# Turning the experts' hidden activations on VectorE instead of TensorE in an encoder layer's expert stage

## The chip, the cores and the metric

The kernel runs on one core of a Trainium2 chip. The metric is the device time of one launch in microseconds (us); lower is better. A core has TensorE (PE, matrix products; PEld is its weight load), VectorE (DVE), ScalarE (ACT), GpSimd (POOL) and SyncE (SP, which here only issues DMAs), each with a queue of its own that it works through in order; queues wait for each other by semaphores.

## The reference

One encoder layer for two groups of 1024 tokens of width 1024 (a mixer, then an expert-choice mixture of experts). The change touches the experts alone:

```python
def expert_choice_moe(h, w_router, w_gate, w_up, w_down):
    ...
    cap = EC_CAPACITY_FACTOR * n // N_EXPERTS          # 128 tokens per expert and group
    gate, idx = lax.top_k(aff.T, cap)
    xe = xf[idx]
    hid = jax.nn.silu(jnp.einsum('ecd,edf->ecf', xe, w_gate)) * jnp.einsum('ecd,edf->ecf', xe, w_up)
    ye = jnp.einsum('ecf,efd->ecd', hid, w_down) * gate[..., None].astype(h.dtype)
    y = jnp.zeros_like(xf).at[idx.reshape(-1)].add(ye.reshape(-1, D))
```

There are 16 experts with three 1024 x 1024 fp32 matrices each. The layer ends with x + gate2 * rmsnorm(y) per token.

## The kernel before

The function `experts` takes the second part of the run, from about 1240 us. Each product of fp32 matrices is made of three products of fp32r matrices: a value is split into a rounded high part and the rest, and hi*hi, hi*lo and lo*hi are added in PSUM. A weight matrix comes in four pieces (`NP`) of 256 rows, 1 MB each; there is one set of four piece buffers (`wf`, `w_hi`, `w_lo`) for all three matrices. SyncE loads a piece as soon as VectorE has split the piece before it in that buffer; ScalarE writes `w_hi` (L2397) as soon as TensorE is through with the piece before; VectorE writes `w_lo` (L2535). A piece is 24 matmuls of 128x128 by 512 columns (2 groups, 2 halves, 2 row blocks, 3 products), an expert 288.

TensorE's order for expert e (L2693 in `products`, body at the end of the file): UP of e, four pieces; the first two GATE pieces of e + 1; `turn_h` of e (L2713); the last two GATE pieces of e + 1; DOWN of e, four pieces. GATE and UP of an expert add into one half of `acc` (4 banks), and `j` switches halves from expert to expert.

The hidden activations `hid` are [token, feature] and must be [feature, token] for DOWN. ScalarE writes silu of GATE's sums into `hid` (L2420), VectorE multiplies UP's sums onto it (`multiply`, L2566). Then `turn_h` makes 16 transposes of 128x128 in four banks (1.75 us in all), ScalarE copies the banks as `h_hi` (L2404, `turned_out`), VectorE subtracts for `h_lo` (L2541). The gathered tokens `xe` take another way: VectorE's 32x32 block transpose (L2550, `turn_x`), with the rows gathered so that no block need change its partitions; it reads every eighth word. They are split at L2410 (ScalarE) and L2555 (VectorE).

VectorE's order in the body of expert e: `turn_x` of e + 1; splits of GATE pieces 1 and 2 of e + 1; `x_out`; GATE pieces 3 and 4; `multiply` of e; DOWN piece 1 of e; `mean` of two units; DOWN piece 2; `turned_out`; `result` of two units; DOWN pieces 3 and 4; UP pieces 1 and 2 of e + 1; `mean` and `result` of two more units; UP pieces 3 and 4. ScalarE's order: the same splits; `square` of two units behind DOWN piece 1; `silu` of e + 1 behind DOWN piece 4; `square` of two more behind UP piece 2; then UP pieces 3 and 4 and `weigh` (L2431, the gated output `ye`). GpSimd then adds `ye` to `y` in memory by a scatter (L2318).

A unit is 128 finished tokens to be normalised and stored: 26 in all. Experts 9 to 14 have four each (`window`), expert 15 two; all others have none. Units use two buffers, `fy` and `fx`, in turn: GpSimd loads two units (L2330, L2331; by indices from unit 16 on, in expert 13 and later, L2334, L2335), ScalarE squares them (L2443), VectorE makes the mean (L2570), GpSimd the root (L2345), VectorE the result (`result`, two instructions, L2578 and L2584), GpSimd stores it (L2352, L2358) and loads the next two only when that store has landed.

Experts 0 to 7 run in a hardware loop, two a pass; the last expert has an order of its own.

Of the kernel before, what the change touches and what calls it, by code (L numbers as in the profile page):

```python
# [5 lines left out]
F32 = mybir.dt.float32  # L6
F32R = mybir.dt.float32r
U32 = mybir.dt.uint32
ALU = mybir.AluOpType
# [2079 lines left out]
def experts(nc, io):  # L2089
# [13 lines left out]
    FIRST, UNITS = 8, 4  # L2103
    units = [(t // TT, t, None) for t in range(GROUPS * TT)]
# [14 lines left out]
    with ExitStack() as ctx:  # L2119
# [35 lines left out]
        h_hi = s.sb("h_hi", [P, GROUPS, KC, P], F32R)  # L2155
        h_lo = s.sb("h_lo", [P, GROUPS, KC, P], F32R)
# [24 lines left out]
        hid_ready = s.sem("hid_ready")  # L2181
        h_turned = s.sem("h_turned")
# [43 lines left out]
        def quarter_rows(g):  # L2226
            return xe[:, g, :].rearrange("p (t n) -> p t n", t=4)

# [161 lines left out]
        def _(act):  # L2390
# [20 lines left out]

            def silu(e, j, bs=range(BK)):
                if bs[-1] < BK - 1:
                    act.wait_ge(half_done, 1)
                else:
                    act.wait_ge(piece_done, ONE + piece(e, GATE, NP))
                if len(bs) == BK:
                    act.wait_ge(h_turned, ONE + e * BK)
                for b in bs:
                    nc.scalar.activation(hid[:, b // 2, b % 2 * HALF:(b % 2 + 1) * HALF], acc[:, j, b, :], ACT.Silu).then_inc(silu_ready, 1)  # L2420
# [36 lines left out]
            def body(e, j):  # L2457

                ns = window(e)
                if is_last(e):  # L2460
                    split(e, DOWN, range(0, 2))
                    turned_out(e, (h_hi, j), h_turned, h_hi_ready, range(0, 2))
                    split(e, DOWN, range(2, NP))
                    for n in ns:
                        square(n)
                    turned_out(e, (h_hi, j), h_turned, h_hi_ready, range(2, BK))
                else:
                    split(e + 1, GATE, range(0, 2))
                    x_out(e + 1, 1 - j)
                    split(e + 1, GATE, range(2, NP))  # L2470

                    split(e, DOWN, range(0, 1))
                    for n in ns[0:2]:
                        square(n)
                    split(e, DOWN, range(1, 2))
                    turned_out(e, (h_hi, j), h_turned, h_hi_ready)
                    split(e, DOWN, range(2, NP))

# [16 lines left out]
        def _(dve):  # L2495
# [61 lines left out]

            def multiply(e, j, bs=range(BK)):
# [42 lines left out]
            def body(e, j):  # L2601
                ns = window(e)
                if is_last(e):
                    multiply(e, j, range(0, 2))
                    split(e, DOWN, range(0, 2))
                    turned_out(e, h_hi, h_lo, j, h_hi_ready, h_ready, range(0, 2))
# [4 lines left out]
                    turned_out(e, h_hi, h_lo, j, h_hi_ready, h_ready, range(2, BK))  # L2611
                    for n in ns:
                        result(n)
                else:
# [50 lines left out]
        def _(pe):  # L2665
# [42 lines left out]
            def turn_h(e, j, bs=range(BK)):  # L2708
                pe.wait_ge(hid_ready, ONE + e * BK + bs[-1] + 1)
                for b in bs:  # L2710
# [3 lines left out]
                    mm.then_inc(h_turned, 1)  # L2714
# [12 lines left out]
            def body(e, j):  # L2727
                first, second = range(0, 2), range(2, NP)
                pe.wait_ge(silu_ready, ONE + e * BK + 2)
                if is_last(e):  # L2730
# [7 lines left out]
                    pe.wait_ge(h_ready, ONE + e * BK + 2)  # L2738
# [3 lines left out]
                    pe.wait_ge(h_ready, ONE + e * BK + BK)  # L2742
                    for b in bs[1]:
                        products(e, DOWN, j, h_hi, h_lo, bs=range(b, b + 1))
                else:
# [7 lines left out]
                    turn_h(e, j)  # L2753
                    products(e + 1, GATE, 1 - j, x_hi[:, 1 - j], x_lo[:, 1 - j], second)
                    pe.wait_ge(h_ready, ONE + e * BK + BK)
                    products(e, DOWN, j, h_hi, h_lo)
# [82 lines left out]
```

## Time and profile before

| | us |
|---|---|
| median of 3 runs | 2374.05 |
| lowest and highest | 2373.64, 2375.26 |
| the profiled execution's own time | 2373.01 |
| its span | 2371.2 |
| TensorE busy | 2267.5 (96%) |
| VectorE busy | 1265.4 (53%) |
| ScalarE busy | 1102.7 (47%) |
| GpSimd busy | 743.5 (31%) |

The span is that of the one profiled execution; its own time holds 1.8 us more around the span. Matmuls are pipelined: a row shows one as busy for 0.39 us while the next starts 0.23 us later, so busy shares of TensorE say little, and the steps between starts are what to read. Idle time of an engine that is not the bottleneck costs nothing by itself.

### The profile page before, as it was taken

The page shows a single profiled execution, that of the slowest core. Times are in us where ns is not written, and L with a number is a line of the kernel's source. Part 1 is how long each engine was busy: PE and PEld are TensorE (multiplying, and loading weights), DVE is VectorE, ACT ScalarE, POOL GpSimd, SP SyncE. Part 2 cuts the span into 40 slices and gives each one's busy share as a digit, 9 for nine tenths or more (in the row PEclk, how much of TensorE's full clock was granted, in tenths as well). Part 3 has the DMA queues.
Part 4 walks back from the last instruction along what each step waited for, and adds up shares of the span by engine and source line. Part 5 has one row for each costly group of instructions (what it writes and reads, how often), then busy time and mean ns, then how long its engine had stood idle before and what let it go on. Part 6 is the DMA issues. An engine that isn't in the chain of part 4 may idle for free. (4 is left out here: it accounts for less than half of the span.)

```text
span 2371.2 us, 34817 instructions
## 1 busy us (share of the span) xinstructions
PE 2267.5 (96%) x13347; PEld 1890.4 (80%) x13347; DVE 1265.4 (53%) x1883; ACT 1102.7 (47%) x1798; POOL 743.5 (31%) x770
## 2 busy tenths in 40 slices
PE   6999999999999999999975999999999999999997
PEld 4679989877899898667754888888888888888886
DVE  3212344555423445656557665555555566777665
ACT  4222444655434436665543444444444445555543
POOL 3004241444132415440013333221223323433634
PEclk9999999999999999999997999999999999999999
DMA  8835445657554459764537667666667679988785
GB/s 317 265 110 181 152 151 187 187 152 175 137 182 152 151 179 258 208 200 157 172 140 283 230 226 230 217 218 210 209 222 235 228 254 325 329 303 302 292 322 177
DMA packets 224095, 511.49 MB, mean 216 GB/s; under 512 B 38420, under 2 KB 129444, under 8 KB 204496
## 3 DMA queue, kind: packets, MB, share of 16 engines
q1 hardware_dynamic: 174576, 394.78, 49.4%
q0 software_dynamic: 49376, 114.78, 16.4%
q8 instruction: 92, 1.51, 0.3%
q14 instruction: 51, 0.42, 0.1%
HBM read 415.32 MB, written 93.69 MB: 215 GB/s over the span
## 5 line engine op out<-in xcount | busy, mean ns | idle before, releaser
L2535 DVE TENSOR_TENSOR moe_w_lo<-moe_wf,moe_w_hi 128x2048 fp32r<-128x2048 f32 x192 | 438.8, 2289 | 369.7 <-ACT moe_w_hi L2397 369.1
L2397 ACT ACTIVATE moe_w_hi<-moe_wf 128x2048 fp32r<-128x2048 f32 x192 | 368.0, 1917 | 524.3 <-PE moe_acc L2693 524.1
L2693 PE MATMUL moe_acc<-moe_w_hi,moe_x_hi 128*128 128x512 f32 x1024 | 400.7, 391 | 0.9 <-DVE moe_x_lo L2541 0.6
L2693 PE MATMUL moe_acc<-moe_w_hi,moe_x_lo 128*128 128x512 f32 x1024 | 399.1, 390 | 0.0
L2693 PE MATMUL moe_acc<-moe_w_lo,moe_x_hi 128*128 128x512 f32 x1024 | 398.9, 390 | 0.0
L2693 PEld LDWEIGHTS moe_acc<-moe_w_hi,moe_x_hi 128*128 128x128 f32 x1024 | 192.3, 188 | 40.8 <-DVE moe_x_lo L2541 0.8
L2693 PEld LDWEIGHTS moe_acc<-moe_w_hi,moe_x_lo 128*128 128x128 f32 x1024 | 192.3, 188 | 40.0
L2693 PEld LDWEIGHTS moe_acc<-moe_w_lo,moe_x_hi 128*128 128x128 f32 x1024 | 192.4, 188 | 39.3
L1793 PE MATMUL banks<-fr_w_hi,fr_h_hi 128*128 128x256 f32 x768 | 223.5, 291 | 0.0
L1793 PE MATMUL banks<-fr_w_lo,fr_h_hi 128*128 128x256 f32 x768 | 217.3, 283 | 0.0
L1793 PE MATMUL banks<-fr_w_hi,fr_h_lo 128*128 128x256 f32 x768 | 217.3, 283 | 0.0
L2301 POOL DMA_INDIRECT moe_xe<-scratch_h,moe_parts x120 | 187.5, 1562 | 85.9 <-issue 76.3
L1784 PE MATMUL banks<-fr_h_hi,fr_w_hi 128*128 128x512 f32 x496 | 204.5, 412 | 1.9 <-DVE fr_h_lo L1381 1.1
L2693 PE MATMUL moe_acc<-moe_w_hi,moe_h_hi 128*128 128x512 f32 x512 | 199.5, 390 | 0.0
L2693 PE MATMUL moe_acc<-moe_w_hi,moe_h_lo 128*128 128x512 f32 x512 | 199.4, 389 | 0.0
L2693 PE MATMUL moe_acc<-moe_w_lo,moe_h_hi 128*128 128x512 f32 x512 | 199.4, 389 | 0.0
L1784 PE MATMUL banks<-fr_h_hi,fr_w_lo 128*128 128x512 f32 x496 | 194.4, 392 | 0.0
L1784 PE MATMUL banks<-fr_h_lo,fr_w_hi 128*128 128x512 f32 x496 | 193.9, 391 | 0.0
L1030 ACT ACTIVATE fr_stage<-banks 128x512 f32<-128x512 f32 (+1 forms) x114 | 67.3, 590 | 272.0 <-PE banks L1784 146.9
L906 POOL DMA_DIRECT2D fr_v<-scratch_vov x224 | 156.5, 743 | 81.6 <-PE banks L1963 80.2
L1362 DVE TENSOR_TENSOR fr_w_lo<-fr_w_raw,fr_w_hi 128x1024 fp32r<-128x1024 f32 x56 | 71.7, 1282 | 206.0 <-ACT fr_w_hi L1018 206.0
L1793 PEld LDWEIGHTS banks<-fr_w_hi,fr_h_hi 128*128 128x128 f32 x768 | 147.0, 191 | 4.9 <-issue 4.8
(303 smaller groups left out, 4191.9 us busy)
## 6 DMA issues: line engine op xcount, KB each, us to landing
moe_wf<-in_w_expert_gate SPq DMA_DIRECT2D x64, 1024.0 KB, 5.0
moe_wf<-in_w_expert_up SPq DMA_DIRECT2D x64, 1024.0 KB, 4.9
moe_wf<-in_w_expert_down SPq DMA_DIRECT2D x64, 1024.0 KB, 6.9
fr_w_raw<-in_w_units SPq DMA_DIRECT2D x28, 1024.0 KB, 6.7
fr_bias<-in_na_bias SPq DMA_DIRECT2D x16, 1520.0 KB, 11.0
fr_a_w<-in_w_ada POOLq DMA_DIRECT2D x16, 1024.0 KB, 8.3
scratch_qk_t<-fr_stage SPq DMA_DIRECT2D x64, 256.0 KB, 2.5
scratch_vov<-fr_stage SPq DMA_DIRECT2D x96, 128.0 KB, 2.4
```

What stands on the lines that cost most here:

```text
L906: pool.dma_start(v[j][p0:CHUNK, CH_AT[rb] + n, :], v_view[2, m, r0:r0 + k, cols_, :]).then_inc(nv_loaded[j], 16)
L1030: nc.scalar.activation(out, product, ACT.Copy).then_inc(evac_done, 1)
L1362: nc.vector.tensor_tensor(w_lo[:, h % 2, k, :], w_raw[:, h % 2, k, :], w_hi[:, h % 2, k, :].bitcast(F32), ALU.subtract).then_inc(w_lo_read ...
L1784: mm = nc.tensor.matmul(ps[:, b % 2, :], w[x1][:, slot, k, a * P:(a + 1) * P], h[x2][:, k, t * HALF:(t + 1) * HALF], start=start, stop=stop)
L1793: mm = nc.tensor.matmul(ps[:, b % 2, part * QW:(part + 1) * QW], h[x1][:, k, tile:tile + P], w[x2][:, slot, k, :], start=(k == 0 and i == ...
L2301: pool.indirect_dma_start(quarter_rows(g)[:, t, :], None, h2_quarters, bass.IndirectOffsetOnAxis(ap=at, axis=0)).then_inc(gathered[g], 16)
L2397: nc.scalar.activation(w_hi[:, q, :, :], wf[:, q, :, :], ACT.Copy).then_inc(w_hi_ready, 1)
L2535: nc.vector.tensor_tensor(w_lo[:, q, :, :], wf[:, q, :, :], w_hi[:, q, :, :].bitcast(F32), ALU.subtract).then_inc(w_lo_ready, 1)
L2693: mm = nc.tensor.matmul(acc[:, j, b, :], x[:, g, k, :], w[:, q, a, h * HALF:(h + 1) * HALF], start=(k == 0 and i == 0), stop=(k == KC - 1 ...
```

## The change

For all experts but the last (`LATE` = 15), `hid` is turned by VectorE with its 32x32 block transpose. Each instruction turns 16 blocks: it reads one quarter of the partitions (32 tokens) and, of each 128 features, one group of 32, and writes them to another quarter of the partitions (the 32 features) of `h_raw`. Sixteen instructions (4 quarters by 4 groups) make the whole, with a drain ahead. `h_raw` lies at the same address as `h_lo`. ScalarE copies it to `h_hi` from SBUF in two instructions of 1024 columns (`h_out`), and VectorE subtracts for `h_lo` in two. `turn_h` of TensorE is gone for these experts. VectorE's order changes: `multiply` moves ahead of the split of GATE's fourth piece, and the turns stand behind that split and ahead of DOWN's first. DOWN's first piece on TensorE is reordered: all its products with `h_hi` first, under a wait for `h_hi` alone, then those with `h_lo`. The last expert keeps the old way under semaphores of its own.

```diff
+    LATE = 15
...
+        with nc.sbuf_tensor("moe_h_raw", [P, GROUPS, KC, P], F32) as h_raw:
+            pass
         h_lo = s.sb("h_lo", [P, GROUPS, KC, P], F32R)
...
             (ScalarE)
+            def h_out(e):
+
+                act.wait_ge(h_turned, ONE + e + 1)
+                for g in range(GROUPS):
+                    nc.scalar.activation(h_hi[:, g, :, :], h_raw[:, g, :, :], ACT.Copy).then_inc(h_hi_ready, 1)
...
                     split(e, DOWN, range(0, 1))
+                    if not is_late(e):
+                        h_out(e)
                     for n in ns[0:2]:
                         square(n)
                     split(e, DOWN, range(1, 2))
-                    turned_out(e, (h_hi, j), h_turned, h_hi_ready)
+                    if is_late(e):
+                        turned_out(e - LATE, (h_hi, j), late_h_turned, late_h_hi_ready)
                     split(e, DOWN, range(2, NP))
...
             (VectorE)
+            def turn_h(e):
+                dve.drain()
+                for t in range(4):
+                    for u in range(4):
+                        columns = hid[t * QT:(t + 1) * QT, :, :].rearrange("r g (m u c) -> r g m u c", m=KC, u=4)[:, :, :, u, :]
+                        a = nc.vector.transpose(h_raw[u * QT:(u + 1) * QT, :, :, t * QT:(t + 1) * QT], columns)
+                a.then_inc(h_turned, 1)
+
+            def h_out(e):
+                for g in range(GROUPS):
+                    dve.wait_ge(h_hi_ready, ONE + e * GROUPS + g + 1)
+                    nc.vector.tensor_tensor(h_lo[:, g, :, :], h_raw[:, g, :, :], h_hi[:, g, :, :].bitcast(F32),
+                                            ALU.subtract).then_inc(h_ready, 1)
...
-                    split(e + 1, GATE, range(2, NP))
-                    multiply(e, j)
+                    if is_late(e):
+                        split(e + 1, GATE, range(2, NP))
+                        multiply(e, j)
+                    else:
+                        split(e + 1, GATE, range(2, 3))
+                        multiply(e, j)
+                        split(e + 1, GATE, range(3, NP))
+                        turn_h(e)
                     split(e, DOWN, range(0, 1))
+                    if not is_late(e):
+                        h_out(e)
                     for n in ns[0:2]:
                         mean(n)
                     split(e, DOWN, range(1, 2))
-                    turned_out(e, h_hi, h_lo, j, h_hi_ready, h_ready)
+                    if is_late(e):
+                        turned_out(e - LATE, h_hi, h_lo, j, late_h_hi_ready, late_h_ready)
                     for n in ns[0:2]:
                         result(n)
...
             (TensorE)
+            def down_first(e, j):
+                pe.wait_ge(w_lo_ready, ONE + piece(e, DOWN, 0) + 1)
+                pe.wait_ge(h_hi_ready, ONE + (e + 1) * GROUPS)
+                for x, ws in ((h_hi, (w_hi, w_lo)), (h_lo, (w_hi,))):
+                    if x is h_lo:
+                        pe.wait_ge(h_ready, ONE + (e + 1) * GROUPS)
+                    for b in range(BK):
+                        for a in range(PIECE):
+                            for w in ws:
+                                mm = nc.tensor.matmul(acc[:, j, b, :], x[:, b // 2, a, :], w[:, 0, a, b % 2 * HALF:(b % 2 + 1) * HALF],
+                                                      start=(a == 0 and w is w_hi and x is h_hi), stop=False)
+                mm.then_inc(piece_done, 1)
...
-                    turn_h(e, j)
+                    if is_late(e):
+                        turn_h(e, j)
                     products(e + 1, GATE, 1 - j, x_hi[:, 1 - j], x_lo[:, 1 - j], second)
-                    pe.wait_ge(h_ready, ONE + e * BK + BK)
-                    products(e, DOWN, j, h_hi, h_lo)
+                    if is_late(e):
+                        pe.wait_ge(late_h_ready, ONE + (e - LATE) * BK + BK)
+                        products(e, DOWN, j, h_hi, h_lo)
+                    else:
+                        down_first(e, j)
+                        products(e, DOWN, j, h_hi, h_lo, range(1, NP))
```

## Rows read from the trace of the kernel before

**Rows 1.** Chain that ended last: start us, us, engine, tile and line.

```profile
1338.76 1.75 PE moe_acc L2713 x16
1340.51 65.33 PE moe_acc L2693 x288
...
2210.59 1.75 PE moe_acc L2713 x16
```

**Rows 2.** Busy time of each engine in two stretches of 67 us.

```profile
1546.00:1613.00 67.00, 67.00 (x306) 55.71 (x305) 38.52 (x26) 31.10 (x26) 17.82 (x13) 1.00 0.67 219
1948.00:2015.00 67.00, 67.00 (x305) 55.72 (x304) 48.54 (x37) 35.72 (x34) 25.50 (x26) 1.00 0.87 314
```

**Rows 3.** Groups by line and shape: count, busy us, mean ns, idle before.

```profile
L2550 DVE STREAM_TRANSPOSE moe_x_raw<-moe_xe 128x1024 f32<-128x1024 f32 x30 | 63.0, 2140 | 0.0
L2541 DVE TENSOR_TENSOR moe_h_lo<-moe_acc,moe_h_hi 128x512 fp32r<-128x512 f32 x64 | 39.7, 683 | 0.3 <-ACT moe_h_hi L2404 0.3
L2555 DVE TENSOR_TENSOR moe_x_lo<-moe_x_raw,moe_x_hi 128x1024 fp32r<-128x1024 f32 x30 | 35.4, 1222 | 0.0
...
L2404 ACT ACTIVATE moe_h_hi<-moe_acc 128x512 fp32r<-128x512 f32 x64 | 32.7, 594 | 0.0
L2410 ACT ACTIVATE moe_x_hi<-moe_x_raw 128x1024 fp32r<-128x1024 f32 x30 | 29.8, 1042 | 0.0
```

**Rows 4.** Timeline around the multiply of expert 3 (start us, us).

```profile
1533.27 2.47 DVE L2566 TENSOR_TENSOR moe_hid<-moe_hid,moe_acc 128x512 f32<-128x512 f32 x4
1536.51 2.29 DVE L2535 TENSOR_TENSOR moe_w_lo<-moe_wf,moe_w_hi 128x2048 fp32r<-128x2048 f32 x1 [0.76 <-ACT moe_w_hi L2397]
```

**Rows 5.** Timelines of ScalarE, VectorE and GpSimd in expert 9.

```profile
1931.56 1.92 ACT L2397 ACTIVATE moe_w_hi<-moe_wf 128x2048 fp32r<-128x2048 f32 x1 [3.52 <-PE moe_acc L2693]
...
1939.00 1.06 ACT L2443 ACTIVATE moe_zero<-moe_fy 128x1024 f32<-128x1024 f32 x1
...
1941.20 0.18 ACT L2443 ACTIVATION_READ_ACCUMULATOR moe_zero<-moe_fy 128x1 f32 x1
...
1948.98 1.28 DVE L2578 SCALAR_TENSOR_TENSOR moe_fy<-moe_fy,moe_parts,moe_rows 128x1024 f32<-128x1024 f32 x1
1950.34 1.23 DVE L2584 TENSOR_TENSOR moe_fx<-moe_fx,moe_fy 128x1024 f32<-128x1024 f32 x1
...
1957.62 0.53 POOL L2330 DMA_DIRECT2D moe_fy<-scratch_y  x1 [1.40 <-DMA out<-moe_fx]
...
1970.96 1.28 DVE L2578 SCALAR_TENSOR_TENSOR moe_fy<-moe_fy,moe_parts,moe_rows 128x1024 f32<-128x1024 f32 x1
```

**Rows 6.** Two lines' instructions: duration ns min/median/max.

```profile
L1661 DVE SCALAR_TENSOR_TENSOR fr_r<-fr_nd x8: 181/187/1301, 268.9 to 873.6; 128x16 f32<-128x16 f32 x8
...
L1575 DVE SCALAR_TENSOR_TENSOR fr_scale<-fr_mods,fr_g_pre x2: 158/163/168, 35.0 to 35.1; 128x8 f32<-128x8 f32 x2
```

**Rows 7.** VectorE's timeline in experts 13 and 14.

```profile
2217.24 1.28 DVE L2578 SCALAR_TENSOR_TENSOR moe_fy<-moe_fy,moe_parts,moe_rows 128x1024 f32<-128x1024 f32 x1
...
2242.43 1.28 DVE L2578 SCALAR_TENSOR_TENSOR moe_fy<-moe_fy,moe_parts,moe_rows 128x1024 f32<-128x1024 f32 x1 [0.91 <-POOL moe_parts L2345]
...
2247.43 4.49 DVE L2535 TENSOR_TENSOR moe_w_lo<-moe_wf,moe_w_hi 128x2048 fp32r<-128x2048 f32 x2
...
2255.92 4.48 DVE L2535 TENSOR_TENSOR moe_w_lo<-moe_wf,moe_w_hi 128x2048 fp32r<-128x2048 f32 x2
...
2284.29 1.28 DVE L2578 SCALAR_TENSOR_TENSOR moe_fy<-moe_fy,moe_parts,moe_rows 128x1024 f32<-128x1024 f32 x1
...
2309.13 1.28 DVE L2578 SCALAR_TENSOR_TENSOR moe_fy<-moe_fy,moe_parts,moe_rows 128x1024 f32<-128x1024 f32 x1
```

**Rows 8.** Transfers of tile `moe_fy`, loads of units.

```profile
DMA to landing us min/median/max: 4.8/8.4/11.1
```

**Rows 9.** Timeline of the end: the last matmul, VectorE behind it.

```profile
2357.03 0.39 PE L2693 MATMUL moe_acc<-moe_w_hi,moe_h_lo 128*128 128x512 f32 x1
...
2357.45 0.75 DVE L2647 SCALAR_TENSOR_TENSOR moe_xe<-moe_acc,moe_parts,moe_xe 128x512 f32<-128x512 f32 x1
```

More of the change, by code:

```diff
@@ L2181, in experts @@
         hid_ready = s.sem("hid_ready")
+        late_h_turned, late_h_hi_ready, late_h_ready = (s.sem(f"late_h_{n}") for n in ("turned", "hi_ready", "ready"))
         h_turned = s.sem("h_turned")
@@ L2227, in quarter_rows, with is_late @@
             return xe[:, g, :].rearrange("p (t n) -> p t n", t=4)
+        def is_late(e):
+            return isinstance(e, int) and e >= LATE
         def is_last(e, n=1):
@@ L2416, in silu @@
                     act.wait_ge(piece_done, ONE + piece(e, GATE, NP))
-                if len(bs) == BK:
-                    act.wait_ge(h_turned, ONE + e * BK)
+                if len(bs) == BK and is_late(e - 1):
+                    act.wait_ge(late_h_turned, ONE + (e - LATE) * BK)
+                elif len(bs) == BK:
+                    act.wait_ge(h_turned, ONE + e)
                 for b in bs:
@@ L2461, in body @@
                     split(e, DOWN, range(0, 2))
-                    turned_out(e, (h_hi, j), h_turned, h_hi_ready, range(0, 2))
+                    turned_out(e - LATE, (h_hi, j), late_h_turned, late_h_hi_ready, range(0, 2))
                     split(e, DOWN, range(2, NP))
@@ L2465, in body @@
                         square(n)
-                    turned_out(e, (h_hi, j), h_turned, h_hi_ready, range(2, BK))
+                    turned_out(e - LATE, (h_hi, j), late_h_turned, late_h_hi_ready, range(2, BK))
                 else:
@@ L2605, in body @@
                     split(e, DOWN, range(0, 2))
-                    turned_out(e, h_hi, h_lo, j, h_hi_ready, h_ready, range(0, 2))
+                    turned_out(e - LATE, h_hi, h_lo, j, late_h_hi_ready, late_h_ready, range(0, 2))
                     multiply(e, j, range(2, BK))
@@ L2610, in body @@
                         mean(n)
-                    turned_out(e, h_hi, h_lo, j, h_hi_ready, h_ready, range(2, BK))
+                    turned_out(e - LATE, h_hi, h_lo, j, late_h_hi_ready, late_h_ready, range(2, BK))
                     for n in ns:
@@ L2713, in turn_h @@
                         mm = nc.tensor.transpose(acc[:, j, b, k * P:(k + 1) * P], hid[:, b // 2, c * P:(c + 1) * P], ident[:, :])
-                    mm.then_inc(h_turned, 1)
+                    mm.then_inc(late_h_turned, 1)
+            def down_first(e, j):
[10 more added lines that the diff above has]
+                mm.then_inc(piece_done, 1)
             bs = [range(2 * g, 2 * g + 2) for g in range(GROUPS)]
@@ L2737, in body @@
                     products(e, UP, j, x_hi[:, j], x_lo[:, j], second, bs[1])
-                    pe.wait_ge(h_ready, ONE + e * BK + 2)
+                    pe.wait_ge(late_h_ready, ONE + (e - LATE) * BK + 2)
                     products(e, DOWN, j, h_hi, h_lo, first, bs[0])
@@ L2752, in body @@
                     products(e + 1, GATE, 1 - j, x_hi[:, 1 - j], x_lo[:, 1 - j], first)
-                    turn_h(e, j)
+                    if is_late(e):
+                        turn_h(e, j)
                     products(e + 1, GATE, 1 - j, x_hi[:, 1 - j], x_lo[:, 1 - j], second)
-                    pe.wait_ge(h_ready, ONE + e * BK + BK)
-                    products(e, DOWN, j, h_hi, h_lo)
+                    if is_late(e):
+                        pe.wait_ge(late_h_ready, ONE + (e - LATE) * BK + BK)
+                        products(e, DOWN, j, h_hi, h_lo)
+                    else:
+                        down_first(e, j)
+                        products(e, DOWN, j, h_hi, h_lo, range(1, NP))
             over_experts(pe, body)
```

## The prediction, made blind

> **What bounds the kernel now.** I read the chain that ended last, then the list of waits, then the timelines of the engines in the experts' stage. From 1339 us to the end TensorE has no wait worth naming: the chain shows 65.3 us of 288 matmuls per expert, 0.227 us each, then 1.75 us for the 16 transposes of `turn_h`, and again; the turns of experts 0 and 13 lie 871.83 us apart, so an expert takes 67.06 us [rows 1]. The stage is bound by how fast TensorE is fed instructions; all else is hidden, or late only from now on. VectorE is the next busiest: 38.5 of 67 us in a plain expert, 48.5 where finished tokens are also normalised (experts 9 to 14, "windows" below) [rows 2].
>
> **What the change removes.** The 16 turns leave TensorE for experts 0 to 14: 15 x 1.75 = 26.2 us, if nothing else becomes late. ScalarE trades four evictions for two copies of 1024 columns, VectorE four subtractions of 512 columns for two of 1024; in time that is even within 0.2 us [rows 3]. No DMA is added. The order of h_hi and h_lo products in the first DOWN piece changes no count of matmuls; it lets h_lo come 16 x 0.227 = 3.6 us later.
>
> **What it adds.** Sixteen VectorE transposes of 32 partitions x 512 columns per expert. Call the time from one start to the next t.
> - Columns set a VectorE duration: 512 take 683 ns, 1024 take 1222, 0.14 us plus 1.06 ns a column [rows 3]. In a run of four, starts lie about 0.60 us apart (2.47 us for four, the last 0.68 long) [rows 4]; where a drain stands between, a 1.28 us instruction is followed after 1.36 [rows 5], so 512 columns would take 0.77.
> - The one transpose row takes 2140 ns for 1024 columns [rows 3], 1.96 ns a column above the same 0.14: for 512, 1.14 us. But it reads every eighth word, where `turn_h` reads runs of 32 words. A read stride alone costs time here: 16 columns read 520 bytes apart take 187 ns, 8 in a dense form 163 [rows 6]; 16 dense ones would take 163 + 8 x 1.06 = 171, so the stride costs 1 ns a column. The transpose's excess over the dense rate is 0.90.
> So t lies between 0.60 and 0.77 at the dense rate, and at 1.14 at the row's own. I take 0.73, nearer the separated end: each transpose writes other partitions than the one before it, and no row shows such a pair overlapping.
>
> The Trainium skill ("VectorE: DVE Perf Modes", section "Two Vector instructions with no wait between them") says that an instruction whose output starts in another group of 32 partitions than the last output did is held until all earlier ones have finished. No run here shows it; by it the overlapped 0.60 is ruled out and t is 0.69 or more, while without it the sum below would be some 11 us lower. The same skill ("SBUF — State Buffer", the note on cachelines) says that reads which cross into a new 16-byte line each time pay a penalty; the transpose row agrees with its 2140 ns, and by it the dense rate holds.
>
> **A plain expert.** Let U be the end of its UP products; ScalarE's next split starts on it (for expert 9 at 1931.56 [rows 5]). VectorE now multiplies at once (2.4), splits the last GATE piece (2.2), drains (0.1), turns (16t), splits the first DOWN piece (2.2). That is U+7.0+16t. TensorE has four GATE pieces until U+21.8. No stall if t is under 0.92; at 0.73 the piece is there at U+18.7, 3 us early. ScalarE's h_hi, 2.0 us after the turns, is earlier still. All 1.75 us are kept: experts 0 to 8 give 9 x 1.75 = -15.7 us.
>
> **Windows.** Here the queue orders matter. Call R1 the start of the first pair of `result`, R2 of the second; between them lies a trip to memory (store the first pair, load into its buffers, square, mean, root). VectorE's order puts R1 behind the turns: multiply, split, turns, then on ScalarE h_hi 2.0, two squares 2.4 [rows 5] and the split of the second DOWN piece 1.9, with 0.1 at each handing over, then VectorE's 2.2. So R1 = U + 4.8 + 16t + 8.7 = U+25.2 at t = 0.73; before it is U+17.5 (1948.98 against 1931.5) [rows 5]. Everything behind R1 on VectorE moves with it, and GpSimd's stores wait for it.
> From R2 to the next R1, VectorE in program order: results 5.0, two splits 4.4, turn_x 4.1, two splits 4.4, x_lo 2.3, split 2.2, multiply 2.4, split 2.2, drain 0.1, turns 16t, then 8.7: 35.8 + 16t [rows 3, 4, 7] (the first step is 2247.43 - 2242.43, the next two 2255.92 - 2247.43 = 8.5 together).
> From R1 to R2, experts 9 to 12: the last load goes out 8.64 us after R1 [rows 5], lands 8.4 later (median) [rows 8], square 1.25, mean, root and their semaphores 1.0: 19.3. Before, VectorE's order hid it (22.0 us). In expert 13 the rows are scattered, and the trip is seen bare: 2242.43 - 2217.24 = 25.2 [rows 7].
> So R1 to R1 is 19.3 + 35.8 + 11.7 = 66.8 us in experts 9 to 12, where TensorE alone would need 65.3 and before took 67.06; and 25.2 + 35.8 + 11.7 = 72.7 from expert 13 to 14, where it took 67.05. TensorE follows, stalled at the third DOWN piece by 1 to 2 us an expert, and behind expert 13's R2 at the third UP piece and at x_lo.
> The end hangs on R1 of expert 14: its R2 comes some 25 us later, then the results' 5.0 and the split of expert 15's third UP piece, 2.2. Before, that piece was there at 2309.13 + 7.2 = 2316.3 [rows 7], and TensorE came to it at 2317.5 (turn of expert 14 at 2210.59 + 67.06, its 1.75, 168 matmuls); that 1 us is all there was to spare. After, R1 is 7.7 us and more later against U and TensorE's way is shorter by the turns: it waits 8 to 9 us. In the end VectorE's queue and the last matmul already meet within 0.2 us (2357.03 + 0.39 and 2357.45) [rows 9], so I let the end move by as much as R1 of expert 14.
>
> **The sum.** Experts 0 to 8 -15.7; R1 of expert 9 later against U by 25.2 - 17.5 = +7.7; four cycles of 66.8 for 67.06, -1.0; the cycle behind expert 13 +5.6. Total -3.4 us. Of 26.2 us won on TensorE the windows give back 23. Against the profiled execution: span 2371.2 - 3.4 = 2367.8, with 1.8 around it 2369.6; the median of the runs lies 1.04 above the profiled time: **2370.7 us**.
>
> **Rivals.**
> 1. *The transposes overlap* (t = 0.60): R1 is U+23.1, +5.6; the cycle would be 64.7, so TensorE's 65.3 rules and four experts give -7.0; expert 13's cycle is 70.6, less the 0.6 spare, +2.9. Sum -14.2: 2360. For it: neighbours on the same partitions overlap [rows 4]. Against: the changing partitions.
> 2. *The trip to memory gets longer*, and the kernel slower. The splits of third and fourth DOWN and first two UP pieces now run back to back, 2.2 us apart instead of 5.4, and each releases a 1 MB load just when the second pair's loads go out. Every us of landing adds 4: from 9.3 us nothing is won, from 10.5 the kernel is slower by 0.2%. At the slowest landing in the rows, 11.1 [rows 8], and t = 0.77: R1 to R1 70.1, four times +3.0; R1 of expert 9 +8.3; expert 13 +6.3; less 15.7: +11.1, 2385. Against: the queues already share the engines now with a median of 8.4.
> 3. *The turns run at the row's own rate*, t = 1.14. First DOWN piece at U+25.2, a stall of 3.4 in each plain expert, 9 x 1.7 = +15; R1 +14.3; four cycles of 73.3, +25; expert 13 +12.3: +67, 2441. For it: it is the only transpose row. Against: the strided rows account for it.
> 4. *The windows cost nothing* because the pair's results are reached in time by slack I don't see: -26.2, 2348. Against: program order on VectorE.
>
> **Chances.** Forecast (dense rate, held, trip as now, -9 to +5) 0.45; rival 1 0.22; rival 2 0.17; rival 3 0.13; rival 4 0.03. Outside 2359 to 2390 are rival 3 and rival 4, 0.16. The forecast's own range is 2365 to 2379. What this kernel's measurement can tell from no change is 0.2%, 4.7 us: faster takes rivals 1 and 4 and a quarter of the forecast, 0.36; same 0.30; slower 0.34.
>
> **What would show it.** The turned group on VectorE: 16 rows, each near 0.69 us, about 11.7 us together (9.6 or 18 for rivals 1 and 3). TensorE: in experts 0 to 8 no wait and starts 65.3 us apart; in windows waits for w_lo of 1 to 2 us; a wait of 8 to 9 us in expert 15's UP. R1 of expert 9 25 us behind U; R1 to R2 19 to 20 us. I am wrong if t is outside 0.69 to 0.77, if the loads' landing shifts by more than 1 us, or if the end follows something other than R1 of expert 14.

## The result and the profile after

The changed kernel takes 2380.87 us (median of 20 runs, 2377.24 to 2386.26); the kernel before took 2374.73 (median of 20, 2372.81 to 2383.17) on the same chips. The ratio is 1.0026 with a 95% interval of 1.002 to 1.0033: slower, just beyond the 0.2% that this measurement tells from no change. The forecast was 2370.7 us, a gain. The profiled execution has a span of 2377.3 us (own time 2379.06) against 2371.2 before, so the traces show 6.1 us to account for.

The chain that ended last, in the plain experts (start us, us, what; L2766 is `down_first`, L2734 all other products):

```profile
1350.73 5.44 PE moe_acc L2766 x24
1356.17 59.84 PE moe_acc L2734 x264
1416.01 5.44 PE moe_acc L2766 x24
...
1872.97 5.44 PE moe_acc L2766 x24
```

No transposes and no waits are left: (1872.97 - 1350.73) / 8 = 65.28 us an expert, where [rows 1] had 67.06. In the plain experts the change does all it promised.

One row of the groups by line, and VectorE's timeline in expert 3, which answer to [rows 3] and [rows 4]:

```profile
L2581 DVE STREAM_TRANSPOSE moe_h_raw<-moe_hid 32x512 f32<-32x512 f32 x240 | 168.7, 703 | 4.5
```

```profile
1524.85 2.48 DVE L2598 TENSOR_TENSOR moe_hid<-moe_hid,moe_acc 128x512 f32<-128x512 f32 x4 [1.14 <-PE moe_acc L2734]
1527.24 2.29 DVE L2553 TENSOR_TENSOR moe_w_lo<-moe_wf,moe_w_hi 128x2048 fp32r<-128x2048 f32 x1
1529.62 11.45 DVE L2581 STREAM_TRANSPOSE moe_h_raw<-moe_hid 32x512 f32<-32x512 f32 x16
1541.10 2.29 DVE L2553 TENSOR_TENSOR moe_w_lo<-moe_wf,moe_w_hi 128x2048 fp32r<-128x2048 f32 x1
1543.31 2.35 DVE L2587 TENSOR_TENSOR moe_h_lo<-moe_h_raw,moe_h_hi 128x1024 fp32r<-128x1024 f32 x2
```

A turn is 703 ns long and the sixteen take 11.45 us, 0.717 from start to start. `h_lo` is complete at 1545.66; TensorE comes to `down_first` at 1546.57, as the chain's steps of 65.28 from 1350.73 give. So even the products with h_lo would not have waited there.

Busy time of each engine in three stretches of 67 us, for [rows 2] (us, PE, PEld, DVE, ACT, POOL busy, granted clock, DMA share, GB/s). The first is plain, the second lies in expert 11's window, the third around expert 13's:

```profile
1545.00:1612.00 67.00, 67.00 (x297) 55.47 (x297) 51.14 (x40) 32.54 (x26) 16.14 (x13) 1.00 0.68 228
2082.00:2149.00 67.00, 63.98 (x280) 52.16 (x280) 56.75 (x49) 33.57 (x32) 26.10 (x26) 1.00 0.83 303
2216.00:2283.00 67.00, 60.84 (x257) 49.49 (x256) 53.58 (x45) 28.20 (x26) 29.76 (x20) 0.95 0.79 288
```

VectorE has 12.6 us more to do in the plain stretch (51.14 for 38.52 [rows 2]) and 8.2 more in the window (56.75 for 48.54), and TensorE now idles 3 to 6 us of 67. In the second row VectorE isn't full; it waits. The DMA engines are busy for 0.83 of it, but full engines alone don't stall TensorE: before, in a window, they were at 0.87 and 314 GB/s [rows 2] and TensorE had no idle time.

The list of waits for TensorE in this stage (engine, tile and line, waited for: us in total, times, longest us):

```profile
PE moe_acc L2734 <- DVE moe_w_lo L2553: 19.7, 7, 9.2
PE moe_acc L2734 <- DVE moe_x_lo L2573: 3.9, 4, 1.8
PE moe_acc L2734 <- ACT moe_hid L2435: 0.3, 1, 0.3
```

Now the trip from the first pair of results (R1) to the second (R2) in expert 11, on the timelines of VectorE, GpSimd and ScalarE:

```profile
2076.10 1.28 DVE L2610 SCALAR_TENSOR_TENSOR moe_fy<-moe_fy,moe_parts,moe_rows 128x1024 f32<-128x1024 f32 x1
...
2084.70 0.53 POOL L2337 DMA_DIRECT2D moe_fy<-scratch_y  x1 [1.03 <-DMA out<-moe_fx]
...
2088.58 1.06 ACT L2458 ACTIVATE moe_zero<-moe_fy 128x1024 f32<-128x1024 f32 x1 [4.36 <-DMA moe_fy<-scratch_y]
...
2096.93 1.06 ACT L2458 ACTIVATE moe_zero<-moe_fy 128x1024 f32<-128x1024 f32 x1 [7.20 <-DMA moe_fy<-scratch_y]
...
2098.12 0.15 DVE L2602 TENSOR_SCALAR moe_parts<-moe_parts 128x1 f32<-128x1 f32 x1 [8.07 <-ACT moe_zero L2458]
2098.19 1.27 DVE L2610 SCALAR_TENSOR_TENSOR moe_fy<-moe_fy,moe_parts,moe_rows 128x1024 f32<-128x1024 f32 x1
```

Read it as a sum: the second fy load goes out 8.60 us behind R1, its square starts 12.23 later (the landing), and R2 comes another 1.26 later: 22.09. ScalarE waits 4.4 and 7.2 us for these loads, VectorE 8.1 us for the square, with TensorE's splits queued behind both. In [rows 5] R2 came 22 us behind R1 too, but there nobody waited for it.

From the same timelines, in us (rows of before: [rows 5] and [rows 7]):

| | expert 9 | 10 | 11 | 12 | 13 | 14 |
|---|---|---|---|---|---|---|
| R1 before | 1948.98 | 2016.04 | 2083.11 | 2150.16 | 2217.24 | 2284.29 |
| R1 after | 1941.33 | 2008.81 | 2076.10 | 2145.30 | 2214.53 | 2288.49 |
| R1 to R2 after | 20.29 | 20.11 | 22.09 | 22.10 | 26.98 | 25.79 |
| R2 to next R1 after | 47.19 | 47.18 | 47.11 | 47.13 | 46.98 | |

The end: TensorE's long wait in expert 15's UP, and the granted clock behind it (timeline; stretches of 5 us as above):

```profile
2321.61 0.80 PE L2734 MATMUL moe_acc<-moe_w_hi,moe_x_hi 128*128 128x512 f32 x1 [9.17 <-DVE moe_w_lo L2553]
```

```profile
2316.00:2321.00 5.00, 0.00 (x0) 0.00 (x0) 4.92 (x4) 4.08 (x5) 1.82 (x1) 0.50 0.26 105
2321.00:2326.00 5.00, 4.39 (x11) 3.48 (x12) 2.76 (x2) 0.00 (x0) 3.56 (x2) 0.52 0.65 217
```

The granted clock is at its lower level, 1.2 GHz, in the last 5 us of the wait of 9.2 us and for about 4 us behind it: the first matmuls start 0.43 us apart where 0.227 is usual. From the matmul above to the transposes of expert 15 lie 48 matmuls; they take 12.98 us, and took 10.89 before.

### The profile page after: what moved, and what is told of

The parts are those of the page before. It is cut to its first block and busy times, and to the rows that moved or that the text cites. A ratio compares the mean times of both kernels' runs of the same rounds, so it can differ in the third digit from the quotient of the medians.

```text
span 2377.3 us, 34487 instructions
## 1 busy us (share of the span) xinstructions
PE 2249.0 (95%) x13107; PEld 1866.4 (79%) x13107; DVE 1424.3 (60%) x2093; ACT 1096.6 (46%) x1768; POOL 730.7 (31%) x770
## 5 line engine op out<-in xcount | busy, mean ns | idle before, releaser
L2734 PE MATMUL moe_acc<-moe_w_hi,moe_x_hi 128*128 128x512 f32 x1024 | 401.7, 392 | 19.0 <-DVE moe_w_lo L2553 14.1
L2734 PE MATMUL moe_acc<-moe_w_hi,moe_x_lo 128*128 128x512 f32 x1024 | 400.2, 391 | 0.0
L2734 PE MATMUL moe_acc<-moe_w_lo,moe_x_hi 128*128 128x512 f32 x1024 | 400.2, 391 | 0.0
L2734 PEld LDWEIGHTS moe_acc<-moe_w_hi,moe_x_hi 128*128 128x128 f32 x1024 | 193.4, 189 | 62.9 <-DVE moe_w_lo L2553 15.9
L2734 PEld LDWEIGHTS moe_acc<-moe_w_hi,moe_x_lo 128*128 128x128 f32 x1024 | 193.2, 189 | 40.5
L2734 PEld LDWEIGHTS moe_acc<-moe_w_lo,moe_x_hi 128*128 128x128 f32 x1024 | 193.4, 189 | 40.0
L2308 POOL DMA_INDIRECT moe_xe<-scratch_h,moe_parts x120 | 177.2, 1476 | 87.1 <-issue 77.5
L1030 ACT ACTIVATE fr_stage<-banks 128x512 f32<-128x512 f32 (+1 forms) x114 | 67.3, 590 | 270.3 <-PE banks L1784 145.4
L2581 DVE STREAM_TRANSPOSE moe_h_raw<-moe_hid 32x512 f32<-32x512 f32 x240 | 168.7, 703 | 4.5
L2734 PE MATMUL moe_acc<-moe_w_hi,moe_h_hi 128*128 128x512 f32 x392 | 153.2, 391 | 5.6 <-DVE moe_w_lo L2553 5.6
L2734 PE MATMUL moe_acc<-moe_w_lo,moe_h_hi 128*128 128x512 f32 x392 | 152.6, 389 | 0.0
L2734 PE MATMUL moe_acc<-moe_w_hi,moe_h_lo 128*128 128x512 f32 x392 | 152.6, 389 | 0.0
```

Of the source, the lines that this page charges most:

```text
L1030: nc.scalar.activation(out, product, ACT.Copy).then_inc(evac_done, 1)
L2308: pool.indirect_dma_start(quarter_rows(g)[:, t, :], None, h2_quarters, bass.IndirectOffsetOnAxis(ap=at, axis=0)).then_inc(gathered[g], 16)
L2581: a = nc.vector.transpose(h_raw[u * QT:(u + 1) * QT, :, :, t * QT:(t + 1) * QT], columns)
L2734: mm = nc.tensor.matmul(acc[:, j, b, :], x[:, g, k, :], w[:, q, a, h * HALF:(h + 1) * HALF], start=(k == 0 and i == 0), stop=(k == KC - 1 ...
```

## The experiments

Twelve kernels were run. Kernels of one group shared a chip and the runs of the kernel before (2374.08, 2374.42 and 2374.44 us in the three groups). Edits are against the changed kernel (2380.87) unless said. The first four ask: is it the windows, the last of them, the order, or the turn itself?

**late9: the turns on VectorE in plain experts alone.**

```diff
-    LATE = 15
+    LATE = 9
```

> The turns stay on VectorE in experts 0 to 8 alone; experts 9 to 14, whose windows normalise finished tokens, turn on TensorE as before. My theory (each plain expert keeps 1.75 us, all of the rest is lost in the windows): 9 x 1.75 = 15.7 us under the kernel before, 2359.0 us, and TensorE's cycle in the windows back at 67.05 us. Rival (the plain experts' gain is given back somewhere else, whatever the windows do, for instance by the loads that now come sooner): within 2 us of the kernel before, about 2375.

Measured: 2358.56 us, ratio to before 0.9934 (0.992 to 0.9948), 15.5 us under the kernel before. R1 of expert 10 and 11 are 2000.61 and 2067.66, 67.05 apart. The theory held: the plain experts' gain is whole, and the windows of the changed kernel lose all of it and 6 us more. One cycle is not back at 67.05: R1 of expert 13 to R1 of expert 14 takes 69.0, though nothing is turned on VectorE there. The next run shows why.

**late14: expert 14 turns on TensorE again** (`LATE = 14`).

> Expert 14 alone turns on TensorE again. Theory: the first pair of results of expert 14 comes some 7.7 us earlier against the end of its UP products, TensorE's 9.2 us wait in expert 15's UP shrinks by that, and TensorE gets 1.75 us of transposes more: 7.4 us under the changed kernel, 2373.5 us, equal to the kernel before. Rival (the end follows TensorE or the loads, not that pair): the turn's 1.75 us are added to the changed kernel, 2382.6.

Measured: 2379.11 us (1.002, 1.0011 to 1.0029). The theory missed by 5.6 us. R1 of expert 14 didn't come sooner: R2 of expert 13 to it takes 47.2 us with a queue that needs some 10 us less. The chain shows what takes that time:

```profile
2252.22 2.52 POOL scratch_y L2325
2255.05 11.63 DMA scratch_y<-moe_ye,moe_parts
2266.94 3.05 POOL moe_fy L2341
2270.29 0.97 POOL moe_fx L2342
2271.56 11.78 DMA moe_fy<-scratch_y,moe_parts
2284.57 1.81 ACT moe_w_hi L2404
2286.41 2.29 DVE moe_w_lo L2553
2289.30 1.79 DVE moe_h_lo L2559 x3
```

GpSimd stores expert 13's second pair, then adds an expert's rows to y (11.6 us), and only then may gather the next window's rows by index (11.8 us). Behind expert 13 a second chain, through GpSimd, is as long as VectorE's queue. My forecast had one chain there, though the chain of the kernel before already ran through the same two transfers:

```profile
2253.69 11.72 DMA scratch_y<-moe_ye,moe_parts
...
2268.24 8.19 DMA moe_fy<-scratch_y,moe_parts
```

**up_first: the second pair behind the last two UP splits**, on both engines; ScalarE's edit, VectorE's is alike:

```diff
-                    split(e + 1, UP, range(0, 2))
+                    split(e + 1, UP)
                     for n in ns[2:4]:
                         square(n)
-                    split(e + 1, UP, range(2, NP))
```

> Order alone is changed: on ScalarE and VectorE the second pair's square, mean and result come behind the splits of UP pieces 3 and 4 in place of ahead of them, so that these two splits (4.4 us on VectorE) fill the trip to memory between the first and the second pair. Theory (the windows lose because VectorE's queue has that trip in it with nothing to do, some 6 to 8 us of idle time each): the cycle falls from 67.3 to 69.2 us to about TensorE's own 65.3 in experts 9 to 12, five cycles give back 2 to 4 us each, and expert 15's third UP piece no longer waits for the results: between 2350 and 2362 us, first results still 25 us behind the end of UP. Rival A (the loads collide with weight loads, and the pair comes later still, whatever stands before it): 2375 to 2381. Rival B (VectorE is simply full with 58 of 65 us, order doesn't matter): 2380.

Measured: 2364.77 us (0.9957, 0.9943 to 0.997), 16 us under the changed kernel and 9 under before; that is 2.8 outside my span, on the theory's side of both rivals. R2 to next R1 is 42.8 in place of 47.2: exactly the two splits, 4.4 us. The trip grew to 23.6 to 24.2, since now the splits themselves wait (ScalarE in expert 11):

```profile
2090.47 1.92 ACT L2404 ACTIVATE moe_w_hi<-moe_wf 128x2048 fp32r<-128x2048 f32 x1 [6.93 <-DMA moe_wf<-in_w_expert_up]
2094.24 1.92 ACT L2404 ACTIVATE moe_w_hi<-moe_wf 128x2048 fp32r<-128x2048 f32 x1 [1.85 <-DMA moe_wf<-in_w_expert_up]
```

The cycles of experts 9 to 12 are 66.4 to 66.9 for 67.3 to 69.2. VectorE has 59 of 67 us of work here and that does no harm: rival B is out. Rival A named a true thing, late loads, and its number is wrong.

**u_outer: neighbouring turns write the same quarter.**

```diff
-                for t in range(4):
-                    for u in range(4):
+                for u in range(4):
+                    for t in range(4):
```

> The two loops of the 16 turns are exchanged: four turns in a row write the same quarter of the partitions, and only three of fifteen neighbours change it (before: all fifteen). The same work, the same result. Theory (a turn waits for the one before it because its output starts in other partitions): starts of neighbours in one quarter 0.60 us apart, the group 9.7 to 10 us instead of 11.45, the first pair of results 1.5 us earlier against U, the kernel 4 to 8 us faster than the changed one, about 2375. Rival (the 0.717 us are what 512 columns of a transpose cost, wherever they go): 11.4 us for the group, 2381.

```profile
1530.99 11.45 DVE L2581 STREAM_TRANSPOSE moe_h_raw<-moe_hid 32x512 f32<-32x512 f32 x16
```

Measured: 2381.71 us (1.0029, 1.0019 to 1.0039); the sixteen again take 11.45 us. Both numbers are the rival's, but the run doesn't decide for it. The exchange moves the change of partitions from one side to the other: in the changed kernel neighbours read the same quarter and write different ones; here they write the same quarter, and each reads another one than its neighbour (`t` is the inner loop). So all fifteen neighbours still differ in partitions on one side. What is shown is that equal output partitions alone bring nothing.

Whether the turns would overlap with equal partitions on both sides stays open, and other rows speak for it. The two transposes of the gathered tokens read and write all partitions, one behind the other (expert 9 of the changed kernel):

```profile
1971.01 2.23 DVE L2568 STREAM_TRANSPOSE moe_x_raw<-moe_xe 128x1024 f32<-128x1024 f32 x1
1973.15 2.13 DVE L2568 STREAM_TRANSPOSE moe_x_raw<-moe_xe 128x1024 f32<-128x1024 f32 x1
```

The second starts 0.09 us before the first ends, and so it is, by 0.06 to 0.11 us, in all 15 pairs. A turn starts 0.013 to 0.014 us after the end of the one before it, in every group, in either loop order. These pairs differ from the turns in shape too, so they are no proof.

The next four look at what lengthens the trip.

**half_w: half the bytes of each weight load from expert 9 on.**

```diff
-                    sp.dma_start(wf[:, q, :, :], mats[step][e, q]).then_inc(w_loaded[q], 16)
+                    if isinstance(e, int) and e > FIRST:
+                        sp.dma_start(wf[:, q, 0:1, :], mats[step][e, q][:, 0:1, :]).then_inc(w_loaded[q], 16)
+                    else:
+                        sp.dma_start(wf[:, q, :, :], mats[step][e, q]).then_inc(w_loaded[q], 16)
```

> A measurement of the disputed transfer, not a version: the changed kernel, but from expert 9 on each weight load brings 512 KB in place of 1 MB (half of every weight piece keeps old values, so the experts' results from there on are others). Instructions, orders and waits are the same. Theory (in the changed kernel the time from the first pair of results to the second is set by the share that weight loads take of the DMA engines, 6.3 MB in the 17 us of it in expert 11 against 4.6 before): the trip falls from 20.1 to 22.1 us to 18 or less in experts 9 to 12, the cycle to 65.3 to 65.5, and the whole to 2366 to 2372. Rival (a bare latency of store, load and square, with no part for the others' bytes): the trips stay within 1 us of 20 and 22, the whole at 2379 to 2381.

One number in that text compares unlike stretches: 4.6 MB is before's traffic at the same clock time. At the same distance from R1 before moved 6.06 MB in 17 us, 2.88 of them on SyncE's queue; the changed kernel 6.30 and 3.37. The whole hardly differs; the weights' part is 0.49 MB more.

Measured: 2361.14 us (0.9943, 0.9924 to 0.9963), 5 under the span of the theory. Trips are 17.9, 17.9, 18.4, 17.9, then 23.6; cycles of experts 9 to 12 are 65.1 to 65.5, TensorE's own. No instruction or wait was taken away, so what moves the trip is the weight loads' traffic. Where it costs the pair's loads their time, in the DMA engines or in memory behind them, no run separates. The stretch around expert 11 (columns as above):

```profile
2082.00:2149.00 67.00, 67.00 (x297) 55.33 (x296) 60.22 (x52) 35.55 (x34) 27.91 (x27) 1.00 0.68 230
```

TensorE never idles with VectorE at 60.2 us of 67 and the DMA share at 0.68 in place of 0.83.

**sp_hold: the next GATE's loads wait for the window's squares.**

```diff
                 if not is_last(e):
+                    if isinstance(e, int) and e > FIRST + 1:
+                        sp.wait_ge(y_sq, UNITS * (e - FIRST - 1))
                     load(e + 1, GATE)
```

> The weight loads of the next GATE are held by SyncE until the window's four squares are done, so that two of them (2 MB) no longer run beside the second pair's loads. Theory (the burst): the trip falls to about 19 us in experts 9 to 12, the kernel by 4 to 8 us to 2373 to 2377. Rival (they are wanted just as soon, and the held loads make the next GATE pieces late): no faster than 2381, with waits of TensorE or ScalarE for wf in GATE.

Measured: 2371.20 us (0.9982, 0.9972 to 0.9992), 9.7 under the changed kernel, beyond the span named. Trips are 20.0, 20.1, 20.8, 19.8, 22.4: the four of experts 9 to 12 give 3.8 us, expert 13's alone 4.6. ScalarE now waits 15.7 us in 8 times for GATE weights, 3.1 at most, and that costs less than it gives.

**fy_first: both fy loads ahead of both fx loads** (`load_unit` takes the part, 0 for fy and 1 for fx, and issues that load alone).

```diff
                     for h, half in enumerate((ns[0:2], ns[2:4])):
-                        for n in half:
-                            load_unit(n)
+                        for part in range(2):
+                            for n in half:
+                                load_unit(n, part)
```

> GpSimd sends both fy loads of a pair ahead of the two fx loads (before: fy, fx, fy, fx). The square needs fy alone. Theory (the trip is a matter of how many bytes stand ahead of the second fy): the second fy lands 1 to 2 us sooner, the trip falls from 20.1 to 22.1 us to 19 to 20.5, five trips give 4 to 8 us: 2373 to 2377. Rival (the second pair's buffer is given free only after the first pair's store, so the order hardly moves the second fy; or fx becomes the late one): 2379 to 2381.

Measured: 2375.92 us (1.0003, 0.9993 to 1.0014), 5 under the changed kernel. The trip fell further than named, to 18.0, 18.1 and 18.0 in experts 9, 10 and 12 (19.1 in 11), but these four cycles stayed at 67.6 to 68.7, together as long as in the changed kernel. VectorE in expert 10 shows why:

```profile
2027.62 1.28 DVE L2610 SCALAR_TENSOR_TENSOR moe_fy<-moe_fy,moe_parts,moe_rows 128x1024 f32<-128x1024 f32 x1
2030.12 1.23 DVE L2616 TENSOR_TENSOR moe_fx<-moe_fx,moe_fy 128x1024 f32<-128x1024 f32 x1 [1.22 <-DMA moe_fx<-scratch_x]
2031.26 1.28 DVE L2610 SCALAR_TENSOR_TENSOR moe_fy<-moe_fy,moe_parts,moe_rows 128x1024 f32<-128x1024 f32 x1
2034.97 1.23 DVE L2616 TENSOR_TENSOR moe_fx<-moe_fx,moe_fy 128x1024 f32<-128x1024 f32 x1 [2.43 <-DMA moe_fx<-scratch_x]
```

fy lands sooner and fx 3.7 us too late. Theory and rival are each half right: the queue's order decides which tile is late. The 5 us come from behind expert 13: its cycle is 72.0 for 74.0, and expert 14's trip 24.4 for 25.8.

**both: up_first, and ScalarE's first pair of squares ahead of its copy of h_hi.**

```diff
-                    if not is_late(e):
-                        h_out(e)
                     for n in ns[0:2]:
                         square(n)
+                    if not is_late(e):
+                        h_out(e)
```

> The second pair behind the splits of UP pieces 3 and 4 (as in up_first, 2364.8 us), and on ScalarE the first pair's squares ahead of the copy of h_hi, in the time in which ScalarE waits for the turns. Theory (ScalarE's two squares, 2.4 us, lie on the way from the turns to the first pair of results): the first results come 2.4 us sooner against the end of UP, 22.6 us behind it in place of 25, VectorE's cycle gets 2.4 us shorter where it bounds: about 2359 to 2362. Rival (with the second pair late, the loads of UP pieces 3 and 4 bound the cycle, as ScalarE's 6.9 us wait for wf in up_first suggests, and they follow the splits in front of the first pair): within 2 us of 2364.8.

Measured: 2362.19 us (0.9939, 0.9924 to 0.9955), 0.2 above the span that I named. It is 2.6 under up_first, but the two intervals overlap, so the times alone don't show that gain; the traces do. R2 to next R1 is 41.6, 1.2 less and not 2.4, since VectorE's own queue now runs from the turns to the first pair with 0.5 us of idle time where it had 1.6; cycles are 66.6, 65.3, 66.1, 65.3, 69.1.

The last four: the other half of the change, a control, and a better version.

**down_plain: DOWN's first piece in the old order.**

```diff
-                        down_first(e, j)
-                        products(e, DOWN, j, h_hi, h_lo, range(1, NP))
+                        pe.wait_ge(h_ready, ONE + (e + 1) * GROUPS)
+                        products(e, DOWN, j, h_hi, h_lo)
```

> The second part of the change alone is undone: DOWN's first piece waits for h_lo and takes its products in the old order. Theory (in the changed kernel h_lo is there 0.9 us before TensorE comes to the first DOWN piece of a plain expert, and in the windows TensorE stalls later, at the third DOWN piece): nothing, 2379 to 2382. Rival (the h_hi products bridge a wait in the windows): 1 us an expert in experts 9 to 14, 2385 and more.

Measured: 2380.68 us (1.002, 1.0009 to 1.003), as the changed kernel. Five waits of at most 0.9 us for h_lo come back (4.3 us together) and move nothing: the waits for `w_lo` shrink from 19.7 to 14.1 us. So this half of the change gains nothing here.

**before_up: the kernel before with up_first's order.**

> Control: the kernel before with only the order of up_first, the second pair's square, mean and result behind the splits of UP pieces 3 and 4. Theory (before, TensorE alone set the 67.05 us of an expert, and the trip to memory was hidden): no gain, 2372 to 2375. Rival (up_first's 16 us are a gain of the order as such, and have nothing to do with the turns): 2358 to 2365.

Measured: 2376.82 us (1.0011, 1.0002 to 1.002): no gain, 0.1% the other way, a little above the span of the theory. Its trips are 30 to 33 us in experts 9 to 12, hidden all the same: TensorE has no wait for VectorE. The 16 us that up_first gave are there only because the trip had become visible.

**late13_both: the orders of both, experts 13 and 14 turned by TensorE** (`LATE = 13`).

> A version to beat both kernels: the orders of both, and experts 13 and 14, whose windows have indexed loads and a trip of 25 to 27 us, turn on TensorE again. Theory (with the orders of both, windows of direct loads cycle near TensorE's 65.3, and only the cycle behind expert 13 and the end were lost): 13 x 1.75 = 22.7 less 1 to 3 us for the first windows, 2353 to 2356. Rival (the chain of GpSimd's indexed stores and loads that held late14 sets the cycle behind expert 13 at 69 to 71 us whoever turns): 2357 to 2360.

Measured: **2355.98 us** (0.9924, 0.991 to 0.9938), 18.5 under before, 25 under the changed kernel, the lowest median here. TensorE's waits from 1300 us to the end are 2.5 us together, and none is for w_lo. Cycles are 66.5, 65.3, 66.2, 62.6, 68.3; the last is near the rival's 69 to 71, the total within the theory's span. But late9, one constant changed, stands at 0.9934 (0.992 to 0.9948): the intervals overlap, and the 2.6 us between the two are not shown to be there.

**late13_both_hold: the same with sp_hold's wait.**

> late13_both, and SyncE holds the next GATE's loads until the window's squares are done (sp_hold alone took 10 us off the changed kernel). Theory (the second pair's loads compete with weight loads here too): 1 to 4 us under late13_both. Rival (with the second pair behind UP's last splits its landing is no longer what VectorE waits for, and held GATE loads come late): 0 to 4 us above it.

Measured: 2372.69 us (0.9985, 0.9976 to 0.9994), 16.7 above late13_both. The rival's direction, at four times its price. Held GATE loads are now late, and so are all loads behind them in SyncE's one queue: ScalarE waits 18.7 us for GATE's wf, 21.4 for DOWN's and 19.6 for UP's (without the hold the twenty longest waits have 16.9 for UP's and neither of the others), GpSimd waits 48.3 us for its adds to y in place of 29.8, and TensorE's list has two waits of 5 us for `h_lo`. Which of these sets the 16.7 us was not taken apart.

## Why the prediction was wrong

| term, us | predicted | measured |
|---|---|---|
| experts 0 to 8 | -15.7 | -16.1 |
| R1 of expert 9 against U | +7.7 | +7.3 |
| four cycles, experts 9 to 12 | -1.0 | +4.9 |
| cycle behind expert 13 | +5.6 | +6.9 |
| behind R1 of expert 14 | 0 | +1.9 |
| start of the stage | 0 | +1.1 |
| sum | -3.4 | +6.1 |

The terms are rounded, the sum is not. The experts' stage began 1.1 us later in this execution (the chain's first matmul behind expert 0's SiLU at 1309.61 for 1308.49), before any turned h is used. U is taken from the start of expert 9's multiply, 1916.53 for 1931.5 before, R1 24.8 behind it.

**Right:** the plain experts; t (0.73 forecast, 0.717 measured); R1 25.2 behind U (24.8); VectorE's queue from R2 to R1 (35.8 + 16t = 47.5, measured 47.0 to 47.2); the wait of 8 to 9 us in expert 15's UP (9.2); that expert 13 is the dearest window. That the windows give back nearly all that TensorE wins was right in kind; they gave back all and 6 us more. The number of t was right, but its reason is neither shown nor refuted, as told below. A slip without weight: by [rows 3] each of ScalarE and VectorE trades its four instructions for two at 0.3 us less, not "even within 0.2".

**The step that failed** is a size: "From R1 to R2, experts 9 to 12: the last load goes out 8.64 us after R1, lands 8.4 later (median)". The first part is near (8.60 in expert 11, 9.1 in 12). The landing is 10.4, 10.2, 12.2 and 11.6 us. What I added behind it, 2.25 us, is 1.3. So trips are 20.3, 20.1, 22.1 and 22.1 for 19.3, and cycles 67.5, 67.3, 69.2 and 69.2 for 66.8: +5.9 us. In expert 13 the trip is 27.0 for 25.2. This is one execution; the profiles of late14, u_outer and down_plain, which change nothing between R1 and R2 of experts 9 to 12, show trips of 21.2 to 22.2 there, so the step fails in them too. It is also one of the prediction's own signs of being wrong: the landing moved by more than 1 us, by 2.7.

Most of the landing's error stood in the trace of before. Its last fy loads alone, in experts 9 to 12 (tile moe_fy, one load each):

```profile
DMA to landing us min/median/max: 9.6/9.6/9.6
...
DMA to landing us min/median/max: 11.1/11.1/11.1
...
DMA to landing us min/median/max: 9.7/9.7/9.7
...
DMA to landing us min/median/max: 9.8/9.8/9.8
```

Their mean is 10.05. The 8.4 of [rows 8] is the median of all sixteen loads, and half of those go out first of their burst: for the step that takes over the path, it was the wrong row. That is 1.65 us of the 2.7 by which the mean landing, 11.1, exceeds 8.4. The other 1.05 came with the change. That part is rival 2, to which I gave 0.17, and its reason, weight loads beside the pair's, is what half_w and sp_hold move: with half the weight bytes the trip is 18, with all of them but later 19.8 to 20.8. Rival 2 had nothing won from 9.3 us of landing on and 0.2% lost from 10.5; the mean of 11.1 is beyond both, and so is the result. With 10.05 its own count would have given about +3 us (-3.4 + 4 x 1.65), no change that can be measured.

**The end's term was wrong by 1.9.** 0.95 of it is expert 14's trip, 25.79 for 24.84 [rows 7]. Behind that, two paths of nearly one length lead to the last result. One is TensorE's: its 48 matmuls behind the long wait take 2.1 us more at the lower clock, less the 1 us that it had to spare. The other is the chain that ended last, which runs through GpSimd from expert 14's second pair on: store it, add rows to y, gather, results of the next pair. It was there before, and the forecast left it out (lines of the chain, before and then after):

```profile
2321.66 10.17 DMA scratch_y<-moe_ye,moe_parts
2332.09 1.52 POOL moe_fy L2334
2345.64 1.28 DVE moe_fy L2578
```

```profile
2326.81 10.51 DMA scratch_y<-moe_ye,moe_parts
2337.57 2.38 POOL moe_fy L2341
2352.02 1.29 DVE moe_fy L2610
```

From R2 of expert 14 to the last of these lines it takes 37.7 us for 36.5. The two paths meet on VectorE at the last matmul:

```profile
2363.80 0.75 DVE L2688 SCALAR_TENSOR_TENSOR moe_xe<-moe_acc,moe_parts,moe_xe 128x512 f32<-128x512 f32 x1 [0.43 <-PE moe_acc L2734]
```

VectorE was free only 0.43 us earlier, so at the full clock behind the long wait the end would have come at most about 0.4 us sooner (an estimate from this row). No run separated the two paths.

**The other rivals.** The transposes don't overlap (rival 1), don't run at the row's own 1.96 ns a column (rival 3), and the windows aren't free (rival 4). The reason that I gave for choosing 0.73 over 0.60, that a change of partitions keeps neighbours apart, stays open. The Trainium skill ("VectorE: DVE Perf Modes", section "Two Vector instructions with no wait between them") says that an instruction whose output starts in another 32 partitions than the last output is held, and so is one whose input starts in another 32 partitions than the last input. By the second half all turns of u_outer are held as before; its unchanged 11.45 us agree with the page, and so do the overlapping transposes of the gathered tokens. The Trainium skill ("SBUF — State Buffer", the note on cachelines) says that reads which cross into a new 16-byte line each time pay a penalty: with runs of 32 words 512 columns take 703 ns, 1.10 ns a column above 0.14 us, and with a stride of eight words 1024 columns take 2140, 1.95 ns a column. That agrees, though the two differ in partitions and output order too.

## What to carry to other kernels

Here moving work to an engine with spare time cost nothing while its queue had no trip to memory in it. Where it has one (a result stored, its buffer loaded again, the next result), the queue's cycle is its own work plus that bare trip, and an engine busy for 57 of 67 us can stall the others. Leave such stages as they are (late9: one constant, 22 us under the changed kernel), or put work that is ready anyway into the trip (up_first: 16 us). And price a transfer that becomes critical by the landing of that very load, the last of its burst, and not by a median over all: then add for the bytes that now run beside it.

## What the runs showed of the hardware that was not expected

- Sixteen VectorE transposes of 32x512 f32 follow each other after 0.717 us (703 ns each), with no overlap, whether neighbours change the quarter of the partitions that they write or the one that they read; two of 128x1024 that keep their partitions overlap by 0.06 to 0.11 us, and so do multiplications of 512 columns in a run, 0.68 us long and 0.60 apart [rows 4].
- With the DMA engines at 0.83 to 0.85 of a 67 us stretch (303 to 312 GB/s), a 512 KB load behind two others lands in 10.2 to 12.2 us. Before the change it was 9.6 to 11.1, at 0.87 to 0.88 and 314 GB/s, so the share over the stretch doesn't give the landing. With half the weight bytes (0.68, 230 GB/s) it is about 8.0, an estimate from the same sum (17.9 - 8.6 - 1.3).
- In the last 5 us of TensorE's wait of 9.2 us, and for 4 us behind it, the granted clock is 0.50 to 0.52; behind one of 4.9 us (at 2248.83) it is 0.62 over the 8 us from 2248; behind waits of 1 to 2 us in the windows it stays at 1.00.
